# The second products of two convolved feed-forward layers, taken by quarters

## What is computed

```python
def conv_ffn(h, w_up, conv_w, conv_b, w_down):
    g, u = jnp.split(h @ w_up, 2, axis=-1)             # 1024 -> 2 x 3072
    g = causal_dwconv(g, conv_w, conv_b)               # three taps along the tokens
    return (jax.nn.gelu(g, approximate=True) * u) @ w_down   # 3072 -> 1024
...
x = x + conv_ffn(rms_norm(x, norm_ffn[layer]), ...)
```

## Time and profile before

| | |
|---|---|
| median of 3 runs | 4195.63 us (4192.86 to 4201.64) |
| the profiled execution | span 4195.6 us |
| TensorE matmuls busy | 4090.6 us, 97% |
| DVE, ACT, POOL busy | 1865.6, 661.3, 1187.6 us |
| `down1`, from the first matmul to the norm's first | 628.00 to 798.07 us |
| `down4`, likewise | 1445.85 to 1615.93 us |

### The profile page before, as it was taken

One profiled execution on the slowest core, in us unless ns is written; L12 is line 12 of the kernel. 1 busy time (PEld: TensorE's weight loads), 2 busy tenths in 40 slices (PEclk: granted clock), 3 DMA queues, 4 the chain that ended last, 5 costly groups with the idle time before them and its releaser, 6 DMA issues. The chain is left out here.

```text
span 4195.6 us, 44153 instructions
## 1 busy us (share of the span) xinstructions
PE 4090.6 (97%) x17518; PEld 2922.0 (70%) x17518; DVE 1865.6 (44%) x3417; ACT 661.3 (16%) x1375; POOL 1187.6 (28%) x1038
## 2 busy tenths in 40 slices
PE   8999999998899999999999999999999989999999
PEld 4448884444488744788844588888888447858888
DVE  4436762347476622443245344334333644434432
ACT  2321110023211101100024310010001321201000
POOL 0004330002344200344403434444442051013443
PEclk9999999999999999999999999999999999989999
DMA  3115443220245442222210122222222242112222
GB/s 128 44 61 182 164 176 136 103 65 31 76 166 188 144 145 85 81 87 82 93 62 24 41 90 82 86 86 81 91 86 76 72 119 54 37 40 81 90 86 76
DMA packets 128780, 387.40 MB, mean 92 GB/s; under 512 B 38208, under 2 KB 41280, under 8 KB 117824
## 3 DMA queue, kind: packets, MB, share of 16 engines
q1 hardware_dynamic: 113936, 306.11, 22.2%
q10 hardware_dynamic: 13824, 75.50, 4.8%
q0 software_dynamic: 816, 2.97, 0.2%
HBM read 376.14 MB, written 8.39 MB: 92 GB/s over the span
## 5 line engine op out<-in xcount | busy, mean ns | idle before, releaser
L828 PE MATMUL bank<-normed,weight_ring 128*128 128x256 f32 (+2 forms) x3312 | 997.1, 454 | 14.7 <-ACT normed L1605 10.0
L828 PEld LDWEIGHTS bank<-normed,weight_ring 128*128 128x128 f32 (+1 forms) x3312 | 622.3, 189 | 354.5 <-issue 273.2
L828 PE MATMUL bank<-area_a,weight_ring 128*128 128x512 f32 (+2 forms) x1744 | 619.7, 511 | 0.3 <-DVE area_a L2602 0.3
L828 PE MATMUL bank<-area_b,weight_ring 128*128 128x256 f32 (+3 forms) x2032 | 598.6, 441 | 4.1 <-issue 2.8
L828 PEld LDWEIGHTS bank<-area_b,weight_ring 128*128 128x128 f32 (+2 forms) x2032 | 378.7, 187 | 184.6 <-issue 146.3
L828 PEld LDWEIGHTS bank<-area_a,weight_ring 128*128 128x128 f32 (+1 forms) x1744 | 328.9, 190 | 254.4 <-issue 233.1
L736 POOL TENSOR_TENSOR area_d<-weight_ring 128x512 f32<-128x512 f32 (+1 forms) x92 | 114.8, 1248 | 1138.1 <-PE bank L828 819.8
L828 PE MATMUL bank<-area_b 128*128 128x256 f32 (+2 forms) x1584 | 345.4, 376 | 13.0 <-DVE area_b L2656 10.5
L828 PEld LDWEIGHTS bank<-area_b 128*128 128x128 f32 (+1 forms) x1584 | 285.9, 191 | 67.6 <-issue 14.9
L828 PE MATMUL bank<-area_b,area_d 128*128 128x256 f32 x1440 | 326.3, 379 | 5.6 <-DVE area_b L2100 5.6
L828 PEld LDWEIGHTS bank<-area_b,area_d 128*128 128x128 f32 x1440 | 273.1, 190 | 44.8 <-issue 7.9
(11 more groups left out here) (304 smaller groups left out, 4808.0 us busy)
## 6 DMA issues: line engine op xcount, KB each, us to landing
weight_ring<-in_weights_dram SPq DMA_DIRECT2D x428, 512.0 KB, 4.6
area_b<-in_weights_dram ACTq DMA_DIRECT2D x48, 1024.0 KB, 4.9
weight_ring<-in_weights_dram SPq DMA_DIRECT2D x35, 1024.0 KB, 4.8
area_b<-in_weights_dram ACTq DMA_DIRECT2D x48, 512.0 KB, 6.4
weight_ring<-in_weights_dram SPq DMA_DIRECT2D x40, 384.0 KB, 4.4
weight_ring<-in_weights_dram SPq DMA_DIRECT2D x25, 256.0 KB, 4.0
low_scratch<-area_d SPq DMA_DIRECT2D x16, 256.0 KB, 2.0
area_d<-low_scratch SPq DMA_DIRECT2D x16, 256.0 KB, 2.8
```

The lines of the kernel that those rows point to most:

```text
L828: i = pe.matmul(out, lhsT, rhs, start=start, stop=stop)
```

## The change

`down1` and `down4` go by quarters too, through the same `down(n)` as the second block's. Each is four steps q (two output blocks), each of three tiles of 16 weight blocks (8 by 2), each of seven parts with four matmuls of 256 columns: 336 of them in place of 192 with 512 columns.

- The order of the first step: P1 of its three tiles, P2 of its three tiles, then P6, P5, P7, P4, P3 of the first tile, of the second and of the third.
- The token sums of the 24 hidden blocks are formed by DVE at the end of `up_gelu`: a first sum in three pieces, around the last taps and the last gated product, then two instructions over all twelve pairs, and a last one in two pieces. They are stored over `normed`, in part of `area_b` and in part of `area_d`.
- The columns of the modulation groups 16 to 23 all go through `ada_group` and bank 7, two groups a step: ahead of P6 of the third tile in the first step, at the start of the third tile in the others. DVE does four `ada_half` (two groups), then both `columns`, then the step's residual.
- ACT: the loads of groups 18 to 23 are issued ahead of each step's copy of P1, two a step; squares go with the copies, as in the second block.
- POOL forms the weight sums of 12 more tiles in each of the two layers.

```diff
-    stage(f"down{n}", DB, 8, DB * FF1)
+    stage(f"down{n}", 0, 0, DB * FF1)
-DOWNS = {6: FF2, 8: FF2, 9: FF2, 11: FF2}
+DOWNS = {1: FF1, 4: FF1, 6: FF2, 8: FF2, 9: FF2, 11: FF2}
...
+def down_parts(n):
+    tiles = len(chunks(DOWNS[n]))
+    order = []
+    for q in range(DB // 2):
+        whole = ("P1", "P2") if q == 0 and n in CONVOLVED else ()
+        order += [(tiles * q + c, what) for what in whole for c in range(tiles)]
+        order += [(tiles * q + c, what) for c in range(tiles) for what in PARTS if what not in whole]
+    return order
...
+        def conv_down_sum(which, i):
+            if which == 0:
+                return h_halves[:, i, :]
+            if which == 1:
+                return b_halves[:, 28 + i, :]
+            return h_halves[:, 12 + i, :] if i < 4 else d_halves[:, i - 4, :]
...
             def ada_group(g):
                 pe.wait_ge(S("ada_summed"), g + 1)
-                if ada_count(g):
-                    pe.wait_ge(S("ada_taken"), ada_count(g))
+                if g:
+                    pe.wait_ge(S("ada_taken"), g)
...
-            def down_conv(n, layer):
-                begin(f"down{n}")
-                name = f"up{n}"
-                hidden = lambda k: part_is_taken(pe, name, k, "MUL")
-                part_is_copied(pe, name, FF1 - 1, "p1")
-                part_is_taken(pe, name, FF1 - 1, "P5")
-                for j in range(DB):
-                    project(lambda k: A[:, k, :], FF1, hidden if j == 0 else settled)
-                    columns(GROUPS * layer + 16 + j)
...
+                for t, what in down_parts(n):
+                    q, c = divmod(t, len(parts))
+                    k, nk = parts[c]
+                    if t not in begun:
+                        begun.add(t)
                         tile_landed(pe, TILE_OF[name, t])
+                        if conv and c == 2 and q:
+                            for e in range(2):
+                                ada_group(GROUPS * CONVOLVED.index(n) + 16 + 2 * q + e)
+                    if conv and t == 2 and what == "P6":
+                        for e in range(2):
+                            ada_group(GROUPS * CONVOLVED.index(n) + 16 + e)
+                    ready = None
+                    if q == 0 and conv and what in ("P1", "P2"):
+                        ready = lambda i: part_is_taken(pe, f"up{n}", k + 2 * i + (what == "P2"), "MUL")
...
+                    if what == "P6":
+                        pe.wait_ge(weight_sums, QUARTER_TILES[name, t] + 1)
...
+                    if t == 0 and conv and what in ("P6", "P7", "P4"):
+                        pe.wait_ge(S("conv_hidden_sums"), at_s + {"P6": 2, "P7": 3, "P4": 4}[what])
+                    if c == 0:
+                        part_is_free(what, *((name, q - 1) if q else (f"up{n}", ff - 1)))
+                    sums = conv_down_sum if conv else lambda j, i: down_sums(ff, j)[:, i, :]
+                    quarter(what, name, t, nk // 2, k // 2, A, sums, c == 0, c == len(parts) - 1, ready)
...
+                add_copies(n, lambda q: [ada_load(GROUPS * layer + 18 + 2 * q + e) for e in range(2) if q < 3])
+            def add_copies(n, between=None):
+                name, tiles = f"down{n}", len(chunks(DOWNS[n]))
+                for q in range(DB // 2):
+                    if between is not None:
+                        between(q)
+                    part_is_full(act, name, tiles * q + tiles - 1, "P1")
+                    if q >= 2:
+                        part_is_taken(act, name, q - 2, "P6")
+                    a(copy_of("p1", q), part_bank("P1"), ACT.Identity).then_inc(part_copied, 1)
+                    if q:
+                        square(n + 1, 2 * q - 2)
+                        square(n + 1, 2 * q - 1)
...
+                first_sums(slice(0, 5))
                 taps(FF1 - 1)
                 for g in groups_after(FF1 - 1):
                     columns(GROUPS * layer + g)
+                first_sums(slice(5, 10))
                 gated(FF1 - 1)
+                every = slice(0, 12)
+                first_sums(slice(10, 12)).then_inc(sem, 1)
+                dve.wait_ge(sem, at_s + 1)
+                tt(of_t(1, every), b22(every), of_t(0, every), ALU.subtract).then_inc(sem, 1)
+                tt(b12(every), b22(every), b12(every), ALU.subtract).then_inc(sem, 1)
+                dve.wait_ge(sem, at_s + 2)
+                for i in (slice(0, 4), slice(4, 12)):
+                    last = tt(of_t(2, i), b21(i), of_t(1, i), ALU.subtract)
+                last.then_inc(sem, 1)
...
+            def add_conv(n, layer):
+                for q in range(DB // 2):
+                    for h in range(32 + 4 * q, 36 + 4 * q):
+                        ada_half(layer, h)
+                    for e in range(2):
+                        columns(GROUPS * layer + 16 + 2 * q + e)
+                    add_quarters(f"down{n}", q, 3 * q + 2, None,
+                                 lambda: (add_square(n + 1, 2 * q - 2), add_square(n + 1, 2 * q - 1)))
```

More of the change, by code:

```diff
@@ L206, in part_order @@
     for n, ff in QUARTERED.items():
-        up, down, tiles = f"up{n}", f"down{n}", len(chunks(ff))
+        up, down = f"up{n}", f"down{n}"
         if n in CONVOLVED:
@@ L217, in part_order @@
             taken[up, ff - 1, "MUL"] = len(taken)
[L218 to L229, removed]
+        else:
+            for p in range(ff):
+                for what in PARTS:
+                    part[up, p, what] = len(part)
+                taken[up, p, "P2"] = len(taken)
+                if p:
+                    taken[up, p - 1, "MUL"] = len(taken)
+                for what in PARTS_TAKEN:
+                    taken[up, p, what] = len(taken)
+                copied[up, p, "p1"] = len(copied)
+                copied[up, p, "act"] = len(copied)
+            taken[up, ff - 1, "MUL"] = len(taken)
+        for t, what in down_parts(n):
+            part[down, t, what] = len(part)
         for q in range(DB // 2):
-            for c in range(tiles):
-                for what in PARTS:
-                    part[down, tiles * q + c, what] = len(part)
             for what in ("P2", *PARTS_TAKEN):
@@ L1003, in down @@
                 parts = chunks(ff)
[L1004 to L1007, removed]
-                        tile_landed(pe, TILE_OF[name, t])
[L1009 to L1017, removed]
-                                part_is_free(what, *((name, q - 1) if q else (f"up{n}", ff - 1)))
-                            quarter(what, name, t, nk // 2, k // 2, A, lambda j: down_sums(ff, j), c == 0,
-                                    c == len(parts) - 1, ready)
+                conv = n in CONVOLVED
@@ L1131, in _ @@
             up(1)
-            down_conv(1, 0)
+            down(1)
             ple(2)
@@ L1212, in _ @@
             up(4)
-            down_conv(4, 1)
+            down(4)
             ple(5)
@@ L1804, in _ @@
             up_gelu(1, 0)
-            norm(2)
+            norm(2, 6)
             def sines():
@@ L1849, in _ @@
             up_gelu(4, 1)
-            norm(5)
+            norm(5, 6)
             ple(5)
@@ L1862, in up_silu @@
                     a(GATE, z_of(p), ACT.Silu).then_inc(part_copied, 1)
-                tiles = len(chunks(ff))
-                for q in range(DB // 2):
-                    part_is_full(act, f"down{n}", tiles * q + tiles - 1, "P1")
-                    if q >= 2:
-                        part_is_taken(act, f"down{n}", q - 2, "P6")
-                    a(copy_of("p1", q), part_bank("P1"), ACT.Identity).then_inc(part_copied, 1)
-                    if q:
-                        square(n + 1, 2 * q - 2)
-                        square(n + 1, 2 * q - 1)
+                add_copies(n)
             norm(6, 6)
@@ L2162, in up_gelu, with of_t, first_sums @@
                     tt(z_of(p)[:, half1], u4, part_bank("P3"), ALU.add).then_inc(part_taken, 1)
+                b11, b12, b21, b22 = (lambda i, e=e, half=half: A[:, 2 * i.start + e:2 * i.stop:2, half]
+                                      for e in range(2) for half in (half0, half1))
+                sem, at_s = S("conv_hidden_sums"), 4 * layer
+                def of_t(which, i):
+                    if which == 0:
+                        return h_halves[:, i, :]
+                    if which == 1:
+                        return b_halves[:, 28 + i.start:28 + i.stop, :]
+                    return h_halves[:, 12 + i.start:12 + i.stop, :] if i.stop <= 4 else d_halves[:, i.start - 4:i.stop - 4, :]
+                def first_sums(i):
+                    part_is_taken(dve, name, 2 * i.stop - 1, "MUL")
+                    return tt(of_t(0, i), b12(i), b11(i), ALU.subtract)
+                first_sums(slice(0, 5))
                 taps(FF1 - 1)
@@ L2338, in _ @@
             up_gelu(1, 0)
-            add("down1")
+            add_conv(1, 0)
             norm(2, lambda k: vec("norm_ple", k))
```

118 lines of the change are left out of this document (52 added, 66 removed).

## The result

The changed kernel takes 4174.79 us at the median of four runs, the kernel before 4194.24 us beside it on the same chip: a ratio of 0.9939 [0.9922, 0.9956]. One of the four took 7881.91 us at a mean granted clock of 0.82 (0.98 to 0.99 in the others); the ratio leaves it out, and the median of the other three is 4171.64 us. The change makes the kernel faster, by some 0.6%. The forecast was 4179 us (4160 to 4190). The profiled execution took 4171.64 us, with a span of 4169.8 us, 25.8 us less than the span before.

A forecast was written before the change was run, and what follows sets the result against it. The changed stages were taken as pure TensorE time. A layer of 149.6 + 1.2 + 5.3 + 5.6 = 161.7 us against 170.1 gains 8.4, two layers 16.8: 4195.6 - 16.8 = 4179 us, range 4160 to 4190.

The forecast's parts named there:

- The matmuls and their pace: Changed layers: 336 matmuls as twelve tiles of 12.08 us, 144.96 us; with columns 149.6 us a layer.
- The columns: Each step's second group waits until DVE has read the first: 0.4 us a step, 1.2 us for three steps.
- The start of the first step: DVE's token sums, in turns with POOL, come late: P6 waits 3.4 us, then a cold start of 1.9; cost 5.3 us.
- The groups of the first step: DVE's group sums, stopped by POOL, make the second group wait 3.65 us, then a cold start of 1.9; cost 5.6 us.
- The rival price in the prediction: Group sums: 0.5 us for each POOL instruction, six costing 3 us, so the second group would wait 0.2 us.
- No turns that matter: Rival at the first step: DVE's sums slip past POOL or POOL begins later; layer 152.0 us, whole 4160; chance 0.27.
- the turns: First step: POOL and DVE instructions alternate, a POOL one holding a two-operand SBUF instruction of DVE up to 1.13 us.
- my case: Both first-step costs occur: layer 161.7 us against 170.1, whole 4179 us; chance 0.56 (4171 to 4187).
- The reserve of the later steps: DVE has 5.7 us to spare before later third tiles; rival: it fails, about 4194 us, no change; chance 0.11.
- TensorE was cold: Rival behind the first step's waits: clock stays down some 35 us instead of 4, about 4210 us; chance 0.06.
- The ring's third tile: First step's third tile, wanted early, is at most 1 us late, which disappears in a longer wait behind it.
- The skill's rule on the lock: DVE instructions with two SBUF inputs and GpSimd ones reading SBUF exclude each other for a whole instruction, not sharing bandwidth.

The follow-up runs named there:

- no_sums: Changed kernel with DVE's token sums for the first step and TensorE's waits for them left out; 0.9907 of the kernel before, a layer 152.5 us.
- p3_early: Changed kernel with P3 of the first step's first two tiles put behind P1 and P2; 0.996 of the kernel before, layers 163.12 and 163.28 us.

## Why the prediction was right

**The matmuls and their pace: right.** I had 144.96 us for the twelve tiles; in `no_sums` the matmuls outside the groups took 145.6, 0.6 us more. The kernel before had the same remainder: eight times 20.60 and 0.58 us are 169.44 of its 170.07, which is 0.63 and not within half a microsecond, as I had it.

**The columns: the term was too small.** I had three trips of 0.4 us, 1.2 us a layer. A pair of groups takes 1.73 us in every step where two groups took 1.16, 0.57 us more: 0.48 for the trip, the rest beside it. Four of them are 2.3 us, and with the 0.6 us of the matmuls they make the 2.9 by which the layer without sums stands above 149.6.

**The start of the first step: right, cause and size.** Predicted 5.3 us (3.4 late, 1.9 cold); measured against `no_sums` 4.8 (3.0 and 1.8) in the first layer and 4.5 in the second, divided otherwise (3.0 at P6, 1.5 at P4). The wait is 3.0 us here and 3.2 by the count above, since P1 and P2 of that step took 10.57 us in `no_sums` and not 24 times 0.431. Without POOL's four instructions the start costs 0.6 us, so the cause is shown.

**The groups of the first step: the term that was mis-sized.** I had 5.6 us, 3.65 of waiting and 1.9 cold. In the first layer it is nothing beyond the trip that every step has; in the second 2.8 us (1.1 and 1.7). Two things failed in this step. I priced one instruction of POOL among the group sums at 1.13 us, the longest stop in the earlier trace rows; a stop costs 0.89 to 1.0, and 0.37 where the instruction falls on a TENSOR_SCALAR. And I let six fall among the sums, not four or five; the high price itself made the chain long enough to meet the last two. Three stops and the smaller one are 3.0 us; six at 1.13 would have been 6.8. The rival price in the prediction, 0.5 us from the median of the earlier trace rows, gave 3 us too, but by luck: it was six instructions at too low a price. A slip that changed nothing: TensorE's first group is 40 matmuls behind 638.4, or 28 behind 643.5, not 40 behind 643.5; both give the 660.9.

The sum by the measured terms, first layer: 149.6 + 2.9 + 4.8 = 157.3 (157.29 measured); second: 149.6 + 2.9 + 4.5 + 2.8 = 159.8 (159.83). Together 23 us gained, not 16.8. At 4171.64 us the whole is 7 us under the forecast, and 6 of these are in the two layers. In the runs after the first the second layer too took 157.3.

**The rivals.** "No turns that matter" named 152.0 us a layer; the turns are there, and without POOL's instructions or DVE's sums it comes to 152.4 to 153.1. The layers as measured lie between that rival and my case: with mine at the start of the first step, nearer to the rival at its groups. The reserve of the later steps did not fail: no wait stands there but the trips. TensorE was cold for two parts or so and not for 35 us. The ring's third tile, which I had let be late by up to 1 us, was late only in some layers of the runs without a long wait behind it, by 0.2 to 0.3 us.

**The skill's rule on the lock.** The Trainium skill (SBUF — State Buffer, "SBUF: two separate sides") says that whichever engine takes the pair first has it for the whole instruction. The long sums of the start agree, both ways round: POOL's instruction of four columns took 1.49 us behind a sum of DVE's of 1.48 us. In the group sums, too, there is one stop for each instruction of POOL that meets a sum of two operands; but it costs 0.89 us, less than the 1.27 of a POOL instruction alone.

## What to carry to other kernels

When you give one late result more cover, look at the next result that TensorE asks for, and at what the new order sets going: `p3_early` took away the wait ahead of P6 and lost 6 us, and the same order gained 5 once the groups were asked for later and in one trip. Price contention by counting the stops, one for each of the holder's instructions that meets one of the held kind: 0.9 to 1.1 us each here, in sums of 0.62 us as in those of 1.48. A mean over a chain hides that some instructions are not held. And when the total scatters by more than the terms do, compare the length of the changed stage, which repeats.

## What the runs showed that was not expected

- The lock holds POOL as well: an instruction of 128x4 elements took 1.49 us (0.21 us just before) while DVE's sum of two SBUF operands ran. A TENSOR_SCALAR of DVE, by contrast, took its 0.60 us inside POOL's 1.47.
- A wait of about 3 us ahead of P6 left TensorE cold in five of the changed kernel's six layers and not in the sixth, with the same code: 2.66 and 2.56 us for the two parts behind it in one, 1.80 us for the first in the other. It was also cold behind waits of 1.48 and 0.76 us with the small matmuls of the groups beside them, and was not in another layer behind the same 1.48 us. What decides this was not tried and stays open; so does a spread of the group sums unevenly over the four steps.
- A trip from TensorE to DVE and back costs 0.48 us, though the reading in it takes 0.15 us.
